# Expert routing by the eight-largest instruction, with fewer rank products and tokens stored in gather order

## The chip, the cores and the metric

The kernel runs on one core of one Trainium2 chip. TensorE multiplies, VectorE and ScalarE (ACT) compute on the fly, GpSimd (POOL) does a few small operations and SyncE (SP) issues nearly all loads. The metric is the device time of one execution in microseconds, the median of three runs.

## The reference

A token block of 256 x 1024 fp32 passes through two layers. The first has a pooling mixer, stick-breaking attention, cross-attention to a memory, gates and a dense feed-forward part. The second has two kinds of attention, gates and a mixture of experts, followed by a last norm. Only the mixture of experts matters here. Each token chooses one of 4 groups, and in that group the two best of 8 experts; its output is the weighted sum of the two.

```python
def hier_moe(h, w_group, b_group, w_expert, b_expert, w1, w3, w2):
    xt = h.reshape(t, d)
    g_logit = (xt @ w_group + b_group).astype(jnp.float32)
    g_prob = jax.nn.softmax(g_logit, axis=-1)
    g_sel = jnp.argmax(g_logit, axis=-1)
    g_w = jnp.take_along_axis(g_prob, g_sel[:, None], axis=1)
    e_logit = (xt @ w_expert + b_expert).astype(jnp.float32).reshape(t, N_GROUPS, EXPERTS_PER_GROUP)
    e_logit = jnp.take_along_axis(e_logit, g_sel[:, None, None], axis=1)[:, 0]
    top_p, top_i = lax.top_k(jax.nn.softmax(e_logit, axis=-1), EXPERT_TOPK)
    gate = g_w * top_p / jnp.sum(top_p, axis=-1, keepdims=True)
    expert = g_sel[:, None] * EXPERTS_PER_GROUP + top_i
    ...
    def expert_block(args):
        xb, e = args
        hid = jax.nn.silu(xb @ w1[e]) * (xb @ w3[e])
        return hid @ w2[e]
    ...
    out = jax.ops.segment_sum(ys[dest] * gate_sorted[:, None], tok_sorted, num_segments=t)
```

There are 32 experts, each with w1 and w3 of 1024 x 512 and w2 of 512 x 1024: three matrices of 2 MB, 192 MB in all.

## The kernel before, in words

Up to about 677 us the kernel works through a list of weight units written by hand (`step_plan`): a unit is loaded by SP, split into a high and a low part, and multiplied in three products (L672 to L674). The mixture of experts follows; all that the change touches lies between these units and the first expert.

Tokens lie on the 128 partitions, in two blocks (`TB`). **Routing.** The "route" steps transpose the last residual times its gain (`n3`, tokens by features) into `n3T`; L853 multiplies it with the 36 routing columns. ACT sums the squares, VectorE adds them up (L1344, L1340), POOL takes the inverse root (L618). VectorE scales the logits (L1686) and then runs one linked chain: each operation waits for the one before it. It finds the best group (helper `first_of`, four operations, which settles ties by the lowest index), hides the other groups' experts, finds the best expert and then the second in the same way, and adds the two masks to `chosen` (L1729), a 0/1 mask of 256 tokens by 32 experts. ACT meanwhile multiplies `n3` by the token's root (L1272, in place) and takes the exponentials of the logits (L1274).

**Ranks.** TensorE, which waits for `chosen` (`route_sel`), counts with five fp32 products how many tokens ahead of each token chose the same expert (`before` is a strict triangle of ones, `ones` a square of ones), and how many tokens each expert has in all (L961 to L965). An fp32 product appears in the trace as two passes, each with a weight load (PEld) and a matmul (PE). VectorE has in the meantime turned the exponentials into gate weights (L1734 to L1743) and then computes `rank` (L1746).

**Experts.** Experts go in quads of four, with 32 slots each. For a quad, VectorE compares ranks with slot numbers into a one-hot matrix (L1768); TensorE gathers the tokens of the quad with 16 fp32 products (L977), whose stationary operand is `n3[:, tb, c:D:KC]`, every eighth feature; ACT and VectorE copy the result to `xg` (L1280, L1778). For each expert TensorE then multiplies with w1 and w3 (L999), transposes (L1004) and multiplies with w2 (L1009); at the quad's end it adds the weighted results into `h` (L1019, L1793). The first quad is written out, the other seven run in a loop. `count_passes` (L1750 to L1753) finds whether an expert has more than 32 tokens and another pass is needed.

**Loads.** SP issues one 2 MB load for each matrix (L560). Experts 0, 1 and 2 are loaded ahead, into places of their own. From expert 3 on, each load waits until the matrix of an earlier expert in the same buffer has been used (`e_w1`, `e_up`, `e_y`), the first of these for expert 0. So the order of work around the change is set by semaphores between five in-order queues, with no planner.

Of the kernel before, what the change touches and what calls it, by code (L numbers as in the profile page):

```python
# [31 lines left out]
P = 128  # L32
# [12 lines left out]
TAKEN = -3e38  # L45
TOPK = T // 4
# [211 lines left out]
def layers_kernel(nc, a, table, windows, out):  # L258
# [32 lines left out]
    gain_rows = [put(f"gain_row{i}", [P, D], F32) for i in range(2)]  # L291
    tab = put("tab", [P, TABLE_W], F32)
# [71 lines left out]
    n3 = nc.alloc_sbuf_tensor_at("n3", [P, TB, D], F32, offset=o_at)  # L364
    n3T = nc.alloc_sbuf_tensor_at("n3T", [P, KC, T], F32, offset=o_at + 8192)
# [16 lines left out]
    masked_e = moe("masked_e", [P, TB, EXPERTS])  # L382
    pick = moe("pick", [P, TB, EXPERTS])
    pick_one = moe("pick_one", [P, TB, EXPERTS])
# [66 lines left out]
    in_route = sem("in_route")  # L451
# [215 lines left out]
    def _(pe):  # L667
# [289 lines left out]
        route_logits(3)  # L957
        pe.wait_ge(route_sel, 1)

        before = const("before")  # L960
# [70 lines left out]
    def _(act):  # L1031
# [270 lines left out]
    def _(dve):  # L1302
# [377 lines left out]
        dve.wait_ge(hg_ready, 4)  # L1680
        dve.wait_ge(sq_ready, 8)
# [11 lines left out]
        def per_token(x, n):  # L1693

            return x.unsqueeze(1).to_broadcast([P, TB, n])

# [3 lines left out]
        def biggest(dst, src, n):  # L1700
            link(v.tensor_reduce(dst, src, AX.X, ALU.max))
# [142 lines left out]
```

## Time and profile before

| | before |
|---|---|
| median of 3 runs | 1166.13 us (1166.05 to 1167.08) |
| the profiled execution | 1163.87 us |
| its span | 1162.0 us |
| mean granted TensorE clock | 0.93 |
| TensorE busy (PE) | 962.2 us, 83% |
| VectorE, ACT, POOL busy | 525.0, 359.8, 46.3 us |
| read from memory | 308.14 MB |

Shares of busy time are means over stages with different limits, so they do not say what bounds the kernel; a matmul's end is modelled. The rows below come from views of the trace of the profiled execution. A row with an idle time in brackets names what ended the wait. A granted clock of 1.00 is 2.4 GHz, 0.50 is 1.2 GHz. The device time is the span and about 2 us around it.

### The profile page before, as it was taken

The page shows a single profiled execution, that of the slowest core. Times are in us where ns is not written, and L with a number is a line of the kernel's source. Part 1 is how long each engine was busy: PE and PEld are TensorE (multiplying, and loading weights), DVE is VectorE, ACT ScalarE, POOL GpSimd, SP SyncE. Part 2 cuts the span into 40 slices and gives each one's busy share as a digit, 9 for nine tenths or more (in the row PEclk, how much of TensorE's full clock was granted, in tenths as well). Part 3 has the DMA queues.
Part 4 walks back from the last instruction along what each step waited for, and adds up shares of the span by engine and source line. Part 5 has one row for each costly group of instructions (what it writes and reads, how often), then busy time and mean ns, then how long its engine had stood idle before and what let it go on. Part 6 is the DMA issues. An engine that isn't in the chain of part 4 may idle for free.

```text
span 1162.0 us, 23578 instructions
## 1 busy us (share of the span) xinstructions
PE 962.2 (83%) x10387; PEld 849.6 (73%) x10387; DVE 525.0 (45%) x859; ACT 359.8 (31%) x541; POOL 46.3 (4%) x43
## 2 busy tenths in 40 slices
PE   5999999889999998999998867767676767676764
PEld 5999999889999987899887866646454545554542
DVE  4546667666565556778875641212020212111112
ACT  4445546453333335343754411010010000001011
POOL 0100001300000000000210200000000000000000
PEclk8999999999999998999999879988898888888887
DMA  9755423736555553455436777999999999999993
GB/s 332 237 170 171 137 73 91 254 130 206 190 180 181 180 182 109 146 156 170 128 128 229 267 301 304 393 420 422 419 422 421 422 422 422 423 423 424 422 421 142
DMA packets 121377, 310.02 MB, mean 267 GB/s; under 512 B 5637, under 2 KB 92361, under 8 KB 113001
## 3 DMA queue, kind: packets, MB, share of 16 engines
q1 hardware_dynamic: 119568, 304.66, 69.9%
q0 software_dynamic: 1008, 4.20, 1.0%
q8 instruction: 43, 0.70, 0.2%
q10 hardware_dynamic: 744, 0.35, 0.1%
q14 instruction: 14, 0.11, 0.0%
HBM read 308.14 MB, written 1.05 MB: 266 GB/s over the span
## 4 chain that ended last, share of the span: by engine, by line
PE 51%; issue 42%; DVE 3%; DMA 2%; ACT 1%; POOL 1%; SPq 0%; ACTq 0%; POOLq 0%; DVEq 0%
PE ps L672 16%; PE ps L674 15%; PE ps L673 15%; DMA arena<-in_w_proj_b 1%; PE ps L927 1%; DVE w_lo L1322 1%; PE ps L838 1%; PE ps L770 0%; PE ps L826 0%; DMA rows<-in_g_mix 0%; PE ps L816 0%; PE ps L805 0%; PE ps L804 0%; DVE h L1412 0%; DVE gates L1488 0%
## 5 line engine op out<-in xcount | busy, mean ns | idle before, releaser
L672 PE MATMUL ps<-x_hi,w_hi 128*128 128x256 f32 x928 | 267.4, 288 | 0.0
L673 PE MATMUL ps<-x_lo,w_hi 128*128 128x256 f32 x928 | 263.4, 284 | 0.0
L674 PE MATMUL ps<-x_hi,w_lo 128*128 128x256 f32 x928 | 263.3, 284 | 0.0
L1322 DVE TENSOR_TENSOR w_lo<-arena,w_hi 128x2048 fp32r<-128x2048 f32 (+3 forms) x83 | 165.5, 1997 | 65.0 <-ACT w_hi L1064 64.3
L999 PE MATMUL ps<-arena,xg 128*32 128x128 f32 x3968 | 137.2, 300 | 62.9 <-DMA arena<-in_w 55.6
L672 PEld LDWEIGHTS ps<-x_hi,w_hi 128*128 128x128 f32 x928 | 178.1, 192 | 5.4 <-issue 4.3
L999 PEld LDWEIGHTS ps<-arena,xg 128*32 128x32 f32 x3968 | 122.8, 121 | 79.7 <-DMA arena<-in_w 66.9
L673 PEld LDWEIGHTS ps<-x_lo,w_hi 128*128 128x128 f32 x928 | 178.1, 192 | 1.6 <-issue 1.0
L674 PEld LDWEIGHTS ps<-x_hi,w_lo 128*128 128x128 f32 x928 | 178.0, 192 | 0.2
L1064 ACT ACTIVATE w_hi<-arena 128x2048 fp32r<-128x2048 f32 (+3 forms) x83 | 138.5, 1671 | 48.9 <-PE ps L674 26.5
L1782 DVE TENSOR_TENSOR hid<-silu_e,ps 128x128 f32<-128x128 f32 x32 | 9.2, 288 | 188.5 <-ACT silu_e L1285 188.5
L1009 PE MATMUL ps<-arena,hid_T 128*32 128x256 f32 x992 | 71.2, 435 | 26.9 <-DMA arena<-in_w 18.8
L672 PE MATMUL ps<-w_hi,x_hi 128*128 128x256 f32 x256 | 76.8, 300 | 11.6 <-DVE w_lo L1322 11.5
L977 PEld LDWEIGHTS ps<-one_hot,n 128*128 128x128 f32 x256 | 61.8, 336 | 25.1 <-DVE one_hot L1768 23.8
L977 PE MATMUL ps<-one_hot,n 128*128 128x128 f32 x256 | 63.3, 424 | 19.2 <-DVE one_hot L1768 19.2
L674 PE MATMUL ps<-w_hi,x_lo 128*128 128x256 f32 x256 | 74.7, 292 | 0.0
L673 PE MATMUL ps<-w_lo,x_hi 128*128 128x256 f32 x256 | 74.7, 292 | 0.0
L1009 PEld LDWEIGHTS ps<-arena,hid_T 128*32 128x32 f32 x992 | 35.6, 123 | 51.9 <-DMA arena<-in_w 23.7
L1787 DVE COPY y_quad<-ps 32x256 f32<-32x256 f32 x64 | 27.2, 425 | 92.9 <-PE ps L1009 91.9
L1332 DVE TENSOR_TENSOR w_lo<-arena,w_hi 128x2048 fp32r<-128x2048 f32 x24 | 55.0, 2293 | 31.2 <-ACT w_hi L1074 31.2
L1285 ACT ACTIVATE silu_e<-ps 128x128 f32<-128x128 f32 x32 | 8.9, 278 | 178.5 <-PE ps L999 178.5
L1288 ACT ACTIVATE y_quad<-ps 32x256 f32<-32x256 f32 x64 | 23.9, 374 | 126.2 <-PE ps L1009 125.4
(274 smaller groups left out, 1330.3 us busy)
## 6 DMA issues: line engine op xcount, KB each, us to landing
arena<-in_w SPq DMA_DIRECT2D x93, 2048.0 KB, 24.0
arena<-in_w_in SPq DMA_DIRECT2D x43, 1024.0 KB, 5.3
arena<-in_w_ffn_in SPq DMA_DIRECT2D x22, 1024.0 KB, 5.1
arena<-in_w_ffn_out SPq DMA_DIRECT2D x11, 1024.0 KB, 4.9
arena<-in_w_out SPq DMA_DIRECT2D x8, 1024.0 KB, 6.1
third_w<-in_w SPq DMA_DIRECT2D x3, 2048.0 KB, 12.6
arena<-in_w_mem_kv SPq DMA_DIRECT2D x2, 1024.0 KB, 5.7
arena<-in_w_pool_o SPq DMA_DIRECT2D x4, 512.0 KB, 3.4
```

The costliest lines, as they stand in the source:

```text
L672: mm(dst, l_hi, r_hi, start=start, stop=False)
L673: mm(dst, l_hi, r_lo, start=False, stop=False)
L674: return mm(dst, l_lo, r_hi, start=False, stop=stop)
L838: mm(o[:, 0:T], v[:, 0, :], r[:, 0:T], start=True, stop=False)
L977: last = mm(ps[:, 2 + c // 4, P * (c % 4):P * (c % 4) + P], n3[:, tb, c:D:KC], one_hot[:, tb, :], start=tb == 0, stop=tb == 1)
L999: last = mm(ps[SLOTS * g:SLOTS * g + SLOTS, 4 + e % 2, P * n:P * n + P], xg[:, c, SLOTS * e:SLOTS * e + SLOTS], places[n][:, c, P * g:P * ...
L1009: last = mm(ps[SLOTS * g:SLOTS * g + SLOTS, 7, 0:UC], hid_T[:, SLOTS * b:SLOTS * b + SLOTS], places[2][:, b, UC * g:UC * g + UC], start=b ...
L1064: fn(w_hi[:, u % 3, 0:n], ring[:, u % 3, 0:n], ACT.Copy).then_inc(hi_ready, 1)
L1288: fn(y_quad[SLOTS * e:SLOTS * e + SLOTS, UC * g:UC * g + UC], ps[SLOTS * g:SLOTS * g + SLOTS, 7, 0:UC], ACT.Copy).then_inc(e_yA, 1)
L1322: v.tensor_tensor(w_lo[:, u % 3, 0:n], ring[:, u % 3, 0:n], w_hi[:, u % 3, 0:n].bitcast(F32), ALU.subtract).then_inc(lo_ready, 1)
L1332: v.tensor_tensor(w_lo[:, s, :], ring[:, s, :], w_hi[:, s, :].bitcast(F32), ALU.subtract)\
L1787: v.tensor_copy(y_quad[SLOTS * e:SLOTS * e + SLOTS, UC * g:UC * g + UC], ps[SLOTS * g:SLOTS * g + SLOTS, 7, 0:UC]).then_inc(e_yD, 1)
```

## The change

- VectorE's chain: the group's mask is turned into 0 or -1e30 and added to the experts' logits. The eight-largest instruction gives each token's best values, the first two are copied into `top2` (padded with -2.5e38), and match-and-replace marks their first places in a copy (`left_e`); a comparison makes `chosen`. The second `first_of` chain is gone. Two memsets for the pads and `slot_no` come ahead of the sum of squares.
- The inputs of the exponential are computed after `chosen`, and the gate weights (`gate_weights`) after the first quad's one-hot.
- TensorE multiplies `ones` by the identity 16 times between the logits and its wait for `chosen`. One rank product covers both token blocks, a second adds the first block's counts to the second's; the two count products come after, in another bank with a semaphore of their own.
- ACT writes the scaled tokens to `n3g`, in the order in which the gather reads its stationary operand. `n3g` lies over columns of the constant table that are no longer needed; `later` changes its place in the table for that. ACT's wait for the transposes (`route_T`) is gone.

```diff
-for _name, _n in (("ident", P), ("later", P), ("before", P), ("rotate", P), ("keep", CAUSAL), ("hide", CAUSAL),
+for _name, _n in (("ident", P), ("before", P), ("later", P), ("rotate", P), ("keep", CAUSAL), ("hide", CAUSAL),
...
+    n3g = nc.alloc_sbuf_tensor_at("n3g", [P, TB, KC, P], F32, offset=tab_at + 4 * TABLE["later"][0])
...
+    masked_e = moe("masked_e", [P, TB, EXPERTS + 6])
+    left_e = moe("left_e", [P, TB, EXPERTS + 6])
+    top2 = moe("top2", [P, TB, 8])
...
         route_logits(3)
+        for _ in range(16):
+            mm(ps[:, 2, 0:P], ones[:, :], ident, start=True, stop=True)
         pe.wait_ge(route_sel, 1)
...
-        mm(ps[:, 1, 0:EXPERTS], before, chosen[:, 0, :], start=True, stop=True)
-        mm(ps[:, 1, EXPERTS:2 * EXPERTS], before, chosen[:, 1, :], start=True, stop=False)
-        mm(ps[:, 1, EXPERTS:2 * EXPERTS], ones[:, :], chosen[:, 0, :], start=False, stop=True)
-        mm(ps[:, 1, 64:64 + EXPERTS], ones[:, :], chosen[:, 0, :], start=True, stop=False)
-        mm(ps[:, 1, 64:64 + EXPERTS], ones[:, :], chosen[:, 1, :], start=False, stop=True).then_inc(rank_done, 1)
+        mm(ps[:, 1, 0:2 * EXPERTS], const("before"), chosen[:, :, :].rearrange("p b e -> p (b e)"), start=True,
+           stop=False)
+        mm(ps[:, 1, EXPERTS:2 * EXPERTS], ones[:, :], chosen[:, 0, :], start=False, stop=True).then_inc(rank_done, 1)
+        mm(ps[:, 5, 0:EXPERTS], ones[:, :], chosen[:, 0, :], start=True, stop=False)
+        mm(ps[:, 5, 0:EXPERTS], ones[:, :], chosen[:, 1, :], start=False, stop=True).then_inc(count_done, 1)
...
-                    last = mm(ps[:, 2 + c // 4, P * (c % 4):P * (c % 4) + P], n3[:, tb, c:D:KC],
+                    last = mm(ps[:, 2 + c // 4, P * (c % 4):P * (c % 4) + P], n3g[:, tb, c, :],
...
         act.wait_ge(root_done, moe_event + 1)
-        act.wait_ge(route_T, 4)
         for tb in range(TB):
-            fn(n3[:, tb, :], n3[:, tb, :], ACT.Copy, scale=stat[:, moe_event, 6 + tb:7 + tb]).then_inc(n3_ready, 1)
+            fn(n3g[:, tb, :, :], n3[:, tb, :].rearrange("t (p c) -> t c p", c=KC), ACT.Copy,
+               scale=stat[:, moe_event, 6 + tb:7 + tb]).then_inc(n3_ready, 1)
...
         dve.wait_ge(hg_ready, 4)
+        v.memset(masked_e[:, :, EXPERTS:], PAD)
+        v.memset(top2[:, :, :], PAD)
+        link(v.tensor_scalar(slot_no[:, :], const("slot"), 1.0, None, ALU.add))
         dve.wait_ge(sq_ready, 8)
...
-        biggest(gmax, lg, GROUPS)
+        link(v.tensor_reduce(gmax, lg, AX.X, ALU.max))
+        tt(pick_g[:, :, :], lg, wide(gmax, GROUPS), ALU.is_equal)
+        tt(pick_g[:, :, :], pick_g[:, :, :], const("revg").unsqueeze(1).to_broadcast([P, TB, GROUPS]), ALU.mult)
+        link(v.tensor_reduce(place, pick_g[:, :, :], AX.X, ALU.max))
+        tt(pick_g[:, :, :], pick_g[:, :, :], wide(place, GROUPS), ALU.is_equal)
+        link(v.tensor_scalar(pick_g[:, :, :], pick_g[:, :, :], 1.0, -NEG, ALU.subtract, ALU.mult))
...
+        tt(real.rearrange("p b (g e) -> p b g e", g=GROUPS), le.rearrange("p b (g e) -> p b g e", g=GROUPS), own,
+           ALU.add)
+        for tb in range(TB):
+            link(v.max(best8[:, tb, :], masked_e[:, tb, 0:EXPERTS]))
+        link(v.tensor_copy(top2[:, :, 0:2], best8[:, :, 0:2]))
+        for tb in range(TB):
+            link(v.match_replace(left_e[:, tb, :], top2[:, tb, :], masked_e[:, tb, :], TAKEN))
+        v.tensor_scalar(chosen[:, :, :], left_e[:, :, 0:EXPERTS], TAKEN / 2 + PAD / 2, None, ALU.is_lt)\
+            .then_inc(route_sel, 1)
+        dve.wait_ge(route_sel, 1)
         tt(exp_in[:, :, 0:GROUPS], lg, wide(gmax, GROUPS), ALU.subtract)
-        first_of(pick_g[:, :, :], lg, gmax, const("revg"), GROUPS, place)
...
-        first_of(chosen[:, :, :], masked_e[:, :, :], best, const("rev"), EXPERTS, place)
...
-        first_of(pick_one[:, :, :], masked_e[:, :, :], second, const("rev"), EXPERTS, place)
-        v.tensor_tensor(chosen[:, :, :], chosen[:, :, :], pick_one[:, :, :], ALU.add).then_inc(route_sel, 1)
-        dve.wait_ge(route_sel, 1)
-        link(v.tensor_scalar(slot_no[:, :], const("slot"), 1.0, None, ALU.add))
...
+        def gate_weights():
...
+            dve.wait_ge(route_exp, 1)
...
         def count_passes():
+            dve.wait_ge(count_done, 1)
...
                 v.tensor_tensor(hot, slots, mine, ALU.is_equal).then_inc(hot_part, 1)
                 dve.wait_ge(hot_part, q * 2 + (tb + 1))
+            if not looped:
+                gate_weights()
```

## Rows read from the trace of the kernel before

**Rows 1.** Page, part 2: the 40 slices of the span, DMA share and rate
```profile
DMA  9755423736555553455436777999999999999993
GB/s 332 237 170 171 137 73 91 254 130 206 190 180 181 180 182 109 146 156 170 128 128 229 267 301 304 393 420 422 419 422 421 422 422 422 423 423 424 422 421 142
```

**Rows 2.** Stretches of the expert stage: us, busy (count) by engine, clock, DMA share, GB/s
```profile
694.00:703.20 9.20, 8.52 (x123) 8.31 (x126) 0.69 (x1) 2.15 (x3) 0.00 (x0) 0.91 0.01 4
749.50:754.00 4.50, 3.31 (x105) 2.79 (x99) 0.58 (x2) 0.28 (x1) 0.00 (x0) 1.00 0.86 277
754.00:1142.50 388.50, 261.89 (x4598) 199.00 (x4587) 64.62 (x162) 32.91 (x93) 0.00 (x0) 0.87 1.01 419
```

**Rows 3.** Waits of the load queue, 676 to 712 us: total, times, longest
```profile
SPq L560 <- PE ps L999: 26.0, 2, 24.6
```

**Rows 4.** Timeline of the routing: start, length, engine, line, form, count, [idle before]
```profile
680.99 0.15 DVE L1344 TENSOR_REDUCE stat<-sq_part 128x2 f32<-128x8 f32 x1
681.13 1.02 PEld L853 LDWEIGHTS ps<-w_route,n3T 128*128 128x128 f32 x8 [1.02 <-DVE n3T L1655]
681.13 1.17 PE L853 MATMUL ps<-w_route,n3T 128*128 128x36 f32 x8 [0.78 <-DVE n3T L1655]
...
681.84 0.70 POOL L618 TENSOR_TENSOR stat<-stat,minus_half 128x2 f32<-128x2 f32 x1 [31.79 <-DVE stat L1340]
682.57 0.55 DVE L1686 SCALAR_TENSOR_TENSOR logits<-ps,stat,b_route 128x36 f32<-128x36 f32 x2 [1.23 <-POOL stat L618]
682.62 2.19 ACT L1272 ACTIVATE n<-n,stat 128x1024 f32<-128x1024 f32 x2 [3.33 <-POOL stat L618]
...
684.83 1.28 ACT L1274 ACT_TABLE_LOAD   x1
...
688.06 0.23 DVE L1729 TENSOR_TENSOR chosen<-chosen,pick_one 128x64 f32<-128x64 f32 x1
...
688.34 0.63 PE L961 MATMUL ps<-chosen,tab 128*128 128x32 f32 x2 [6.04 <-DVE chosen L1729]
688.53 0.16 DVE L1734 TENSOR_REDUCE r_s<-exp_out 128x2 f32<-128x8 f32 x1
...
690.06 0.61 PE L965 MATMUL ps<-chosen,ones 128*128 128x32 f32 x2
...
690.81 0.22 DVE L1746 SCALAR_TENSOR_TENSOR rank<-ps,chosen 128x64 f32<-128x64 f32 x1
691.07 0.62 DVE L1768 TENSOR_TENSOR one_hot<-slot_no,rank 128x128 f32<-128x128 f32 x2
...
691.83 7.88 PE L977 MATMUL ps<-one_hot,n 128*128 128x128 f32 x32 [1.15 <-DVE one_hot L1768]
...
699.75 0.60 ACT L1280 ACTIVATE xg<-ps 128x512 f32<-128x512 f32 x1 [13.37 <-PE ps L977]
```

**Rows 5.** Vector operations by shape: count, busy us, mean ns
```profile
L1673 DVE MAX8 best<-work 128x8 f32<-128x128 f32 x8 | 2.3, 286 | 0.0
L1674 DVE MATCH_REPLACE8 work<-best,work 128x128 f32<-128x128 f32 x8 | 2.2, 276 | 0.0
...
L1552 DVE MEMSET ones<- 128x128 f32 x1 | 0.2, 165 | 0.8 <-PEq L1831 0.8
```

**Rows 6.** Stretches of the routing and of the first gather, columns as in Rows 2
```profile
682.00:688.30 6.30, 0.30 (x2) 0.15 (x1) 4.96 (x24) 3.73 (x4) 0.54 (x1) 0.50 1.00 426
691.80:695.65 3.85, 3.82 (x16) 3.85 (x17) 1.06 (x6) 0.00 (x0) 0.00 (x0) 0.50 0.46 186
695.65:699.70 4.05, 4.05 (x20) 4.04 (x19) 0.00 (x0) 0.00 (x0) 0.00 (x0) 1.00 0.00 0
```

**Rows 7.** Timeline of the second quad, columns as in Rows 4
```profile
739.49 7.91 PE L977 MATMUL ps<-one_hot,n 128*128 128x128 f32 x32 [2.42 <-DVE one_hot L1768]
...
750.53 38.13 SPq L560 DMA_DIRECT2D arena<-in_w  x12
...
789.31 3.67 PE L1019 MATMUL ps<-y_quad,gate_T 128*128 128x512 f32 x8 [1.11 <-DVE y_quad L1787]
```

More of the change, by code:

```diff
@@ L45 @@
 TAKEN = -3e38
+PAD = -2.5e38
 TOPK = T // 4
@@ L1710, in _ @@
-        gmax, place, gsum, best, second, total, share = (r_s[:, i, :] for i in range(7))
-        lg, le = logits[:, :, 0:GROUPS], logits[:, :, GROUPS:36]
-        biggest(gmax, lg, GROUPS)
-        tt(exp_in[:, :, 0:GROUPS], lg, wide(gmax, GROUPS), ALU.subtract)
-        first_of(pick_g[:, :, :], lg, gmax, const("revg"), GROUPS, place)
-        own = pick_g[:, :, :].unsqueeze(3).to_broadcast([P, TB, GROUPS, PER_GROUP])
-        dst, hidden = (t[:, :, :].rearrange("p b (g e) -> p b g e", g=GROUPS) for t in (masked_e, pick))
@@ L1718, in _ @@
-        tt(dst, le.rearrange("p b (g e) -> p b g e", g=GROUPS), own, ALU.mult)
-        link(v.tensor_scalar(hidden, own, 1.0, -NEG, ALU.subtract, ALU.mult))
-        tt(dst, dst, hidden, ALU.add)
-        biggest(best, masked_e[:, :, :], EXPERTS)
-        v.tensor_tensor(exp_in[:, :, GROUPS:36], masked_e[:, :, :], wide(best, EXPERTS), ALU.subtract)\
-            .then_inc(route_in, 1)
-        first_of(chosen[:, :, :], masked_e[:, :, :], best, const("rev"), EXPERTS, place)
-        link(v.scalar_tensor_tensor(masked_e[:, :, :], chosen[:, :, :], 2 * NEG, masked_e[:, :, :], ALU.mult,
-                                    ALU.add))
@@ L1736, in _ @@
-        link(v.tensor_reduce(total, exp_out[:, :, GROUPS:36], AX.X, ALU.add))
-        link(v.reciprocal(total, total))
-        tt(gate_e[:, :, :], exp_out[:, :, GROUPS:36], wide(total, EXPERTS), ALU.mult)
-        tt(gate_e[:, :, :], gate_e[:, :, :], chosen[:, :, :], ALU.mult)
-        link(v.tensor_reduce(share, gate_e[:, :, :], AX.X, ALU.add))
-        link(v.reciprocal(share, share))
-        tt(share, share, gsum, ALU.mult)
-        tt(gate_e[:, :, :], gate_e[:, :, :], wide(share, EXPERTS), ALU.mult)
+        gmax, place, gsum, _, _, total, share = (r_s[:, i, :] for i in range(7))
@@ new lines, in _ @@
+        own = pick_g[:, :, :].unsqueeze(3).to_broadcast([P, TB, GROUPS, PER_GROUP])
+        real = masked_e[:, :, 0:EXPERTS]
+        tt(real.rearrange("p b (g e) -> p b g e", g=GROUPS), le.rearrange("p b (g e) -> p b g e", g=GROUPS), own,
[5 more added lines that the diff above has]
+            link(v.match_replace(left_e[:, tb, :], top2[:, tb, :], masked_e[:, tb, :], TAKEN))
@@ L1747, in _ @@
                                     ALU.mult))
+        def gate_weights():
+            dve.wait_ge(route_exp, 1)
+            link(v.tensor_reduce(gsum, exp_out[:, :, 0:GROUPS], AX.X, ALU.add))
+            link(v.reciprocal(gsum, gsum))
+            link(v.tensor_reduce(total, exp_out[:, :, GROUPS:36], AX.X, ALU.add))
+            link(v.reciprocal(total, total))
+            tt(gate_e[:, :, :], exp_out[:, :, GROUPS:36], wide(total, EXPERTS), ALU.mult)
+            tt(gate_e[:, :, :], gate_e[:, :, :], chosen[:, :, :], ALU.mult)
+            link(v.tensor_reduce(share, gate_e[:, :, :], AX.X, ALU.add))
+            link(v.reciprocal(share, share))
+            tt(share, share, gsum, ALU.mult)
+            tt(gate_e[:, :, :], gate_e[:, :, :], wide(share, EXPERTS), ALU.mult)
         def count_passes():
-            link(v.tensor_reduce(r_s[:, 8, 0:1], ps[:, 1, 64:64 + EXPERTS], AX.X, ALU.max))
+            dve.wait_ge(count_done, 1)
+            link(v.tensor_reduce(r_s[:, 8, 0:1], ps[:, 5, 0:EXPERTS], AX.X, ALU.max))
             link(v.tensor_scalar(exp_in[:, 0, 0:8], const("steps"), r_s[:, 8, 0:1], None, ALU.is_lt))
```

22 lines of the change are left out of this document (4 added, 18 removed).

## The prediction

> **What bounds the kernel now.** I read the 40 slices first, then the waits of the load queue, then the stretches around the one hole they show, and last the timeline of that hole. From slice 27 to slice 39 the memory rate stands near 420 GB/s in nearly every slice [rows 1]: the expert stage lives on its stream of weights. Over its long part, 754.0 to 1142.5 us, the stream moves 419 GB/s at a DMA share of 1.01 while TensorE is busy 262 of 388.5 us [rows 2]. An engine made faster there is worth nothing. What counts is when the stream starts and where it stands still. It stands still once for long: from 694.0 to 703.2 us it moves 4 GB/s [rows 2]. The reason is in the load queue: its longest wait, 24.6 us, is for the up-projection of the first expert (L999) [rows 3]. Experts 0 to 2 were loaded ahead; expert 3 needs the buffers of expert 0, which are free only when routing and first gather are over and expert 0 has run. So every microsecond by which the first gather ends earlier moves the whole stream, as long as the hole is not used up: 9.2 us are there. There is a second, small hole, 749.5 to 754.0 us, at 277 GB/s [rows 2]: the queue waits for the first expert of the second quad, behind that quad's gather [rows 7].
>
> The chain to shorten is therefore [rows 4]: the token statistics (L1344, L618), the vector chain to `chosen` (ready at 688.06 + 0.23 = 688.29), the rank products on TensorE (688.34 to 690.06 + 0.61 = 690.67), rank and one-hot on VectorE (690.81 to 691.69), the gather (from 691.83, 7.88 us), and the copies of its result (from 699.75).
>
> **The change, part by part.** All times are those of the profiled execution: 1163.87 us, of which 1162.0 us are span. The median of the three timed runs is 1166.13, 2.26 us more; I carry the difference over unchanged.
>
> *New work ahead of the statistics.* Two memsets and `slot_no` are now ahead of L1344 on VectorE. L1344 started at 680.99 with nothing between it and the copy before it, so POOL's root and everything behind it move. A memset of 128 columns takes 0.165 us [rows 5]; at most 3 times that, 0.5. They are pure additions, so no gain is possible, and 0 is the other end. I take 0.5: logits start at 683.05 in place of 682.57.
>
> *The vector chain.* Before, from the first logits (682.57) to `chosen` (688.06) lie 23 starts: 0.24 us each [rows 4]. Now two logits are followed by 13 operations: one maximum over groups, four for the group, one turned into a mask, one addition, two eight-largest, one copy, two match-and-replace, one comparison. An eight-largest over 128 columns takes 0.286 and a replace 0.276 [rows 5], over 32 and 38 columns hardly more than the 0.24 of a step; the replace has a separate value load, for which I add 0.1 in all. 14 steps of 0.24, plus 0.23, plus 0.1 make 3.7: `chosen` is ready at 686.75, 1.5 us earlier. At 128-column prices for all four it would be about 0.2 later.
>
> *Sixteen warm-up products on TensorE.* TensorE's queue is in order, so the rank products stand behind them, and the gather behind those. They start when the logit products end, 681.13 + 1.17 = 682.3 [rows 4]. Each is two passes, 32 in all. At 2.4 GHz a pass of this kind takes 0.12 (eight loads in 1.02 us, less the tail of the last) [rows 4]; 128 columns streamed do not take longer (eight products of 512 columns in 3.67 us [rows 7], 0.46 each, a quarter is 0.115). At 1.2 GHz it takes 0.215 (eight passes from 688.34 to 690.06) [rows 4]. So the warm-ups end between 682.3 + 3.8 = 686.1 and 682.3 + 6.9 = 689.2. From 682.0 the granted clock is 0.50, that is 1.2 GHz; TensorE then stood nearly idle, and the clock was full only from 695.65, after 3.85 us of gather [rows 6]. I carry this delay over: 17.7 slow passes until 686.1, the other 14.3 fast in 1.7, end at 687.8. That is after `chosen` (686.75), so about 1.05 us of the vector chain's gain is lost in this queue; a later `chosen` would cost nothing up to there.
>
> *Rank.* Two products (4 passes, 0.5 at 2.4 GHz, 0.86 at 1.2) in place of five before the rank is read: 688.3. The count products come after it; the number of passes is needed only at the end of the first quad. From the last rank product to VectorE's start it took 0.14, from there to the gather 1.02 [rows 4]: the gather starts at 689.45 in place of 691.83, 2.4 us earlier.
>
> *The gather.* Its weights were every eighth element of a token's row; now they are contiguous. Before, 32 passes took 7.88 us, 0.24 each, and the pace did not follow the clock: 3.85 us at 0.50 and 4.05 us at 1.00 hold about the same number of records, 16 and 20, of the latter two already the transposes behind it [rows 6]. So the stride set the pace, not the clock. Contiguous, I take 0.12, in all 3.8 us: 4.1 us gained. Bounds: nothing (another cause of the 0.24), and 4.1.
>
> *Who writes that order.* ACT's two copies (2.19 us, from 682.62) now read with the stride and write in a row. At the old price they end at 685.3, table load at 686.6. The gather asks for them at 689.45. The bound from above is the factor that the stride cost TensorE, 0.24 to 0.12, twice: 4.4 us, end at 687.5. Hidden by 1.9 us. Dropping the wait for the transposes is worth nothing, since the root comes later. The table's columns that are overwritten are no longer read.
>
> The Trainium skill speaks here against the change: "SBUF — State Buffer" (section "Door 1: The DMA port swizzle", its note on cachelines) says that SBUF is read in lines of 16 bytes and that each access to a new line pays, so for fp32 a stride beyond 4 elements costs. The gather's pace agrees with it; that the same penalty meets ACT's copies is not shown by any row of before. If it were twofold, the time would be the same as by the row.
>
> *Moved work.* The exponential is fed two steps after `chosen`, 687.25, and ends near 687.5 behind the table load. The ten gate operations (688.53 to 690.81, 2.3 us [rows 4]) now come behind the one-hot, from 689.3; with the two gated one-hots and the four of the pass count VectorE is free at about 693.0, and the gather ends at 689.45 + 3.8 = 693.25. Covered, but only by 0.25 us: if the gather is faster than I think, its result waits here. No DMA issue is moved and none is passed by another.
>
> *Sum.* 2.4 + 4.1 = 6.5 us, less than the 9.2 us of the hole, so it passes in full to the stream. Second quad: the small hole costs (419 - 277) x 4.5 / 419 = 1.5 us of stream [rows 2]. The second gather (7.91 us [rows 7]) gets 1.0 us shorter if all passes are slow, 4.1 if all are fast, 2.4 with the clock's delay of 3.85 us: 1.5 of it closes the hole. In the other six quads the stream covers it. Together 8.0 us: 1155.9 in a profiled execution, **1158.1** against the median.
>
> The clock alone moves this. With the warm-ups ending at 686.1, `chosen` governs, and the gather starts at about 688.5: 0.95 more. With an end at 689.2 it starts at about 690.85: 1.4 less. Its own range is thus 1157.0 to 1159.7. The Trainium skill, "TensorE: Matmul & The Clock Gate", Part 1, holds that the number of slow products after a start differs between runs of one kernel; one profiled execution can't show that.
>
> **The rivals.**
> *The clock stays at 1.2 GHz.* Warm-ups to 689.2, ranks in 0.86, gather from 691.2 and in 6.9 us: ends at 698.1 in place of 699.71, 1.6 gained, and 1.0 in the second quad. Time: 1163.5. For it: after the five rank products the clock was still at 0.50. Against it: a solid stretch brought it back, after 3.85 us [rows 6].
> *The new order does not quicken the gather.* The 0.24 would then be a matter of the product itself. 2.4 are gained: 1163.7. Against it: the 0.12 of the other products on the same data width.
> *The stream gives it back.* If later stretches are limited by something other than the bytes, the earlier start ends in a longer wait: 1166.1, no change. Against it: 419 GB/s over 388 us.
> *Slower: ACT's strided copies.* The mechanism is their reading; the place is TensorE's wait for both ahead of the first gather. From 689.45 on they delay the gather one for one. The whole 8.0 us are lost when they end at 697.5, 14.4 us after their start at 683.1, 7.2 us for one copy in place of 1.1; at 8.6 us for one it is 1169.0. For it: no row shows ACT reading such a stride. Against it: the same stride cost TensorE a factor of two.
>
> **How the numbers follow.** Forecast 0.70; slow clock 0.11; gather not quicker 0.09; given back 0.06; slower 0.04. From all of this I can tell only what exceeds 0.2%, 2.3 us. The forecast is faster; of the two rivals at 2.6 and 2.4 us of gain about two thirds, 0.14, would be told as faster; the rest and the third are the same. So faster 0.84, same 0.12, slower 0.04. The range reaches from the forecast's fast end, with half a microsecond for the tail behind the last load, to the slow clock: 1156.4 to 1163.5.
>
> **What would show it.** The chain right: gather start near 689.5 and passes near 0.12 at full clock; the hole of 9.2 us shrunk to about 2.7; no stretch near 277 GB/s in the second quad; the same 419 GB/s after it. Wrong: warm-ups that end after 689 at clock 0.50; passes still at 0.24; ACT's copies over 3 us each; VectorE still in the gate weights when the gather ends; a hole that opens at a later quad.

## The result and the profile after

The changed kernel takes 1158.28 us in the median of five runs (1152.85 to 1159.67), the kernel before 1166.13 (1165.64 to 1167.08): a ratio of 0.9929 with an interval of 0.9905 to 0.9954. The forecast was 1158.1. The runs of the changed kernel lie 6.8 us apart, those of before 1.4 (in the later comparisons, of 16 or 17 runs, 4.4 to 6.8), and the profiled execution is the changed kernel's lowest, 1152.85 us with a span of 1151.0. The trace therefore shows more gain than the median, and the difference has to be explained too.

Page after, part 2, answering to [rows 1]. The dip before the plateau is nearly gone; the plateau is the same.

```profile
DMA  9754423746555553545444889999999999999993
GB/s 334 226 184 142 152 67 109 229 137 209 183 182 182 184 186 113 160 142 167 147 145 154 288 327 367 419 419 422 422 421 421 422 421 422 423 423 423 421 423 152
```

Stretches after, answering to [rows 2, 6]: start:end, length, busy (count) of PE, PEld, DVE, ACT, POOL, granted clock, DMA share, GB/s.

```profile
681.50:684.70 3.20, 3.20 (x16) 3.20 (x16) 1.87 (x10) 2.12 (x2) 0.70 (x1) 0.50 0.99 425
684.90:692.40 7.50, 6.89 (x63) 6.80 (x61) 5.24 (x28) 3.48 (x3) 0.00 (x0) 1.00 0.98 409
693.20:696.20 3.00, 2.88 (x107) 2.91 (x111) 0.02 (x1) 1.41 (x2) 0.00 (x0) 1.00 0.10 36
705.20:736.00 30.80, 23.35 (x453) 17.72 (x457) 8.17 (x20) 3.66 (x10) 0.00 (x0) 1.00 1.01 421
736.00:743.00 7.00, 5.81 (x173) 4.91 (x168) 1.42 (x4) 1.03 (x3) 0.00 (x0) 1.00 1.01 408
743.00:1131.50 388.50, 250.50 (x4517) 180.96 (x4506) 63.14 (x158) 32.08 (x91) 0.00 (x0) 0.86 1.01 420
```

The hole of 9.2 us at 4 GB/s is now one of 3.0 us at 36. The second hole, 277 GB/s before, is gone (408). The stream behind it is the same, 420 against 419. The load queue's longest wait fell accordingly, from 24.6 us [rows 3] to this one (total, times, longest):

```profile
SPq L564 <- PE ps L1004: 28.3, 4, 17.6
```

Timeline of the routing after, answering to [rows 4]: start, length, engine, line, form, count, [idle before].

```profile
680.92 0.16 DVE L1349 TENSOR_REDUCE stat<-sq_part 128x2 f32<-128x8 f32 x1
...
682.03 5.16 PE L963 MATMUL ps<-tab,ones 128*128 128x128 f32 x32
682.52 0.55 DVE L1694 SCALAR_TENSOR_TENSOR logits<-ps,stat,b_route 128x36 f32<-128x36 f32 x2 [1.23 <-POOL stat L622]
682.58 4.26 ACT L1276 ACTIVATE n3g<-n,stat 128x1024 f32<-128x1024 f32 x2 [3.60 <-POOL stat L622]
...
684.56 0.42 DVE L1718 MAX8 best<-masked_e 128x8 f32<-128x32 f32 x2
...
685.81 0.20 DVE L1722 TENSOR_SCALAR chosen<-left_e 128x64 f32<-128x64 f32 x1
...
687.02 0.33 PE L966 MATMUL ps<-chosen,tab 128*128 128x64 f32 x2
...
687.59 0.22 DVE L1730 SCALAR_TENSOR_TENSOR rank<-ps,chosen 128x64 f32<-128x64 f32 x1 [1.12 <-PE ps L968]
...
688.61 3.81 PE L982 MATMUL ps<-one_hot,n3g 128*128 128x128 f32 x32 [0.61 <-DVE one_hot L1767]
...
691.88 0.15 DVE L1752 CAST passes_i<-r_s 128x1 int32<-128x1 f32 x1
...
692.46 0.60 ACT L1285 ACTIVATE xg<-ps 128x512 f32<-128x512 f32 x1 [4.04 <-PE ps L982]
692.53 0.69 DVE L1779 COPY xg<-ps 128x512 f32<-128x512 f32 x1 [0.49 <-PE ps L982]
...
695.33 2.07 SPq L564 DMA_DIRECT2D arena<-in_w  x2
```

The last line is the first load of expert 3, at 695.33. VectorE was done with the gate weights 0.49 us before the gather ended.

**A clock that two executions share.** The work up to the loads of expert 2 (`third_w`, issued by SP) is the same in both kernels, yet it ends at 673.98 to 678.99 us in the 14 profiles of this case. I therefore count from that issue, t0: 676.72 before, 676.42 after. The table gives, in us after t0, when each event starts (the end of the span in the last column); "last w2 product" is the last group of products with a w2 matrix.

| kernel | gather starts | its copies | w1 of expert 3 | last w2 product | end |
|---|---|---|---|---|---|
| before | 15.11 | 23.03 | 25.90 | 465.80 | 485.28 |
| before, again | 15.11 | 23.03 | 25.90 | 465.75 | 485.15 |
| changed | 12.19 | 16.04 | 18.91 | 456.60 | 474.58 |
| changed, again | 12.20 | 16.05 | 18.91 | 456.65 | 474.71 |
| changed, third | 12.19 | 16.04 | 18.90 | 460.55 | 478.56 |

Within a kernel the routing and the gather come at the same time to 0.01 us; between the kernels they differ by 7.0 us. What follows varies more.

### The profile page after: what moved, and what is told of

Same layout as the page of the kernel before. It is cut to its first block, busy times and chain, and to the rows that moved or that the text cites. A ratio compares the mean times of both kernels' runs of the same rounds, so it can differ in the third digit from the quotient of the medians.

```text
span 1151.0 us, 23634 instructions
## 1 busy us (share of the span) xinstructions
PE 948.4 (82%) x10417; PEld 829.9 (72%) x10417; DVE 522.5 (45%) x856; ACT 361.5 (31%) x541; POOL 46.3 (4%) x43
## 4 chain that ended last, share of the span: by engine, by line
PE 52%; issue 41%; DVE 3%; ACT 1%; DMA 1%; POOL 1%; ACTq 0%; POOLq 0%; DVEq 0%; SPq 0%
PE ps L676 16%; PE ps L677 15%; PE ps L678 15%; PE ps L931 1%; DMA arena<-in_w_proj_b 1%; DVE w_lo L1327 1%; PE ps L842 1%; PE ps L830 0%; PE ps L774 0%; DMA rows<-in_g_mix 0%; PE ps L820 0%; PE ps L809 0%; PE ps L808 0%; DVE h L1417 0%; DVE gates L1493 0%
## 5 line engine op out<-in xcount | busy, mean ns | idle before, releaser
L1004 PE MATMUL ps<-arena,xg 128*32 128x128 f32 x3968 | 141.4, 306 | 66.2 <-DMA arena<-in_w 60.2
L1004 PEld LDWEIGHTS ps<-arena,xg 128*32 128x32 f32 x3968 | 125.4, 124 | 86.6 <-DMA arena<-in_w 75.2
L1014 PE MATMUL ps<-arena,hid_T 128*32 128x256 f32 x992 | 76.3, 457 | 35.4 <-DMA arena<-in_w 29.6
L676 PEld LDWEIGHTS ps<-w_hi,x_hi 128*128 128x128 f32 x256 | 52.0, 203 | 14.6 <-DVE w_lo L1327 12.2
L1079 ACT ACTIVATE w_hi<-arena 128x2048 fp32r<-128x2048 f32 x24 | 45.8, 1910 | 49.9 <-PE ps L678 49.9
```

The lines of the kernel that those rows point to most:

```text
L676: mm(dst, l_hi, r_hi, start=start, stop=False)
L1004: last = mm(ps[SLOTS * g:SLOTS * g + SLOTS, 4 + e % 2, P * n:P * n + P], xg[:, c, SLOTS * e:SLOTS * e + SLOTS], places[n][:, c, P * g:P * ...
L1014: last = mm(ps[SLOTS * g:SLOTS * g + SLOTS, 7, 0:UC], hid_T[:, SLOTS * b:SLOTS * b + SLOTS], places[2][:, b, UC * g:UC * g + UC], start=b ...
L1079: fn(w_hi[:, s, :], ring[:, s, :], ACT.Copy).then_inc(hi_ready, 1)
```

## The experiments

Each kernel below is the changed one with one edit, or the one before with one part of the change. Kernels that were timed together share one set of runs of the kernel before. Its median is 1164.19 for the changed kernel again, the order undone, the first version without warm-ups and the order alone; 1164.41 for the delay, the first early version and the repetitions of the changed kernel and of the one without warm-ups; 1164.49 for the other four.

### The changed kernel again

No edit.

> The changed kernel once more, for a second profile and five more times. Its first profile has a span of 1151.0 us, while the other four runs have spans of 1155.6 to 1157.9. If the stream theory holds in the ordinary run too, the first gather ends near 692.4 and the hole of the load stream is near 3 us in this profile also; a longer span must then show a second place where the stream stands still or TensorE waits (candidate: waits marked 'issue' in the first quad, of which before had 2.8 us and the first profile of after 0.6 us). Rival: the spread comes from the clock, and the warm-ups end later, near 689. Median 1157 to 1159.

Measured: median 1155.51 of 6 (1151.07 to 1158.47), ratio 0.992 (0.9899 to 0.9941). The gain is 8.7 us here, 7.85 in the first comparison; the chain comes at the same times after t0. The spread of some 7 us is there again.

### The gather's order undone

```diff
-                    last = mm(ps[:, 2 + c // 4, ...], n3g[:, tb, c, :],
+                    last = mm(ps[:, 2 + c // 4, ...], n3[:, tb, c:D:KC],
...
+        act.wait_ge(route_T, 4)
...
-            fn(n3g[:, tb, :, :], n3[:, tb, :].rearrange("t (p c) -> t c p", c=KC), ACT.Copy,
...
+            fn(n3[:, tb, :], n3[:, tb, :], ACT.Copy, ...
```

> The changed kernel with the tokens left in n3 and gathered with the stride again; all else as changed. Stream theory: the first gather takes 7.9 us in place of 3.8, the whole stream is 4.1 us later, the second quad's hole reopens (about 1.5 us): near 1163.9, that is 5.6 above the changed kernel. Rival (the earlier routing carries the gain, the gather is hidden by the stream): within 1.5 us of the changed kernel.

Measured: median 1161.01 of 12 (1155.36 to 1163.3), ratio 0.9963 (0.9948 to 0.9978). Timeline of this kernel, then its stretch of the gather:

```profile
682.73 2.19 ACT L1277 ACTIVATE n<-n,stat 128x1024 f32<-128x1024 f32 x2 [3.58 <-POOL stat L622]
...
688.78 7.86 PE L982 MATMUL ps<-one_hot,n 128*128 128x128 f32 x32 [0.61 <-DVE one_hot L1767]
```

```profile
688.80:696.60 7.80, 7.80 (x34) 7.80 (x34) 2.93 (x16) 0.00 (x0) 0.00 (x0) 1.00 0.61 246
...
738.00:750.00 12.00, 10.05 (x217) 8.92 (x220) 2.08 (x5) 1.89 (x5) 0.00 (x0) 1.00 1.01 418
```

At full clock throughout the strided gather takes 7.86 us, as before with half of it at 0.50. So the stride sets its pace, not the clock. Against the changed kernel's first profile the order is worth 4.05 us at the gather's end (20.09 against 16.04 after t0), at expert 3's load (22.96 against 18.91), at the last product (460.65 against 456.60) and 4.1 at the end. I had added the second hole to the order's account; in this kernel that hole is closed as well (418 GB/s), with the strided gather. So the order isn't what closes it. The faster routing need not be either: TensorE has none of the idle stretches in the first quad that the kernel before has there (1.29 and 1.54 us, below). The medians lie 5.5 us apart, and the intervals of the two ratios don't meet (0.9948 and more here, 0.9941 and less there).

### The warm-ups left out, twice

```diff
-        for _ in range(16):
-            mm(ps[:, 2, 0:P], ones[:, :], ident, start=True, stop=True)
```

> The changed kernel without the 16 warm-up products. The rank products then start when chosen is ready (686.05) at 1.2 GHz, 4 passes in 0.86, and the gather at about 688.1, half a us earlier than with warm-ups, but slow until the clock returns 3.85 us later: 17.7 passes at 0.215 and 14.3 at 0.12, end near 693.6 against 692.4. Clock theory: 1.2 us slower than the changed kernel, near 1159.5. Rival (the warm-ups are only a delay in TensorE's queue): 0.5 us faster. Second rival (the clock stays low through the first expert too): 4 us slower or more.

> One more look at the kernel without the 16 warm-ups. Its first profile had the third experts' loads at 674.0, the first load of expert 3 20.1 later (18.9 with warm-ups) and the end 478.6 later (474.7 with them), with waits marked 'issue' of 1.21, 0.42 and 0.16 in the first quad and a stretch at 1.2 GHz there. If the warm-ups are worth 4 us in the stage, this profile again has 478 to 479 from these loads to the end. Rival (the 4 us were a chance of the clock): 475 to 476.

Stretches of the first profile without warm-ups (its first gather, then two places in the first quad), then the first gather of its repetition:

```profile
685.70:689.30 3.60, 3.56 (x17) 3.59 (x18) 2.91 (x15) 0.17 (x1) 0.00 (x0) 0.53 1.00 408
689.30:691.20 1.90, 1.90 (x19) 1.83 (x17) 0.16 (x2) 0.01 (x1) 0.00 (x0) 1.00 0.77 313
706.00:709.50 3.50, 3.50 (x49) 2.47 (x45) 0.51 (x2) 0.52 (x2) 0.00 (x0) 0.52 1.01 413
711.00:714.00 3.00, 2.00 (x68) 1.47 (x56) 0.20 (x1) 0.28 (x1) 0.00 (x0) 1.00 0.81 198
```

```profile
689.40:693.20 3.80, 3.80 (x18) 3.80 (x19) 3.07 (x16) 0.11 (x1) 0.00 (x0) 0.51 0.99 399
693.20:695.00 1.80, 1.80 (x18) 1.77 (x17) 0.00 (x0) 0.00 (x0) 0.00 (x0) 1.00 0.74 303
```

The ranks come 1 us earlier (9.65 after t0, not 10.60), the gather's first 17 passes are slow, and it takes 5.41 and 5.61 us; its copies start 1.2 and 1.4 us later than with warm-ups. So much was expected. Behind it, t0 to end is 478.6 in both profiles, 4.0 more than in two of the changed kernel's three profiles and the same as in its third. Of the 4.0, 2.3 and 2.4 are there when the last w2 product starts (458.94 and 459.04); the rest is that product itself, which takes 3.55 and 3.45 us and not 1.93. The share ahead of that product is more than the gather's 1.2 and 1.4: in the first quad the clock is at 0.52 for 3.5 us, and behind it the stream falls to 198 GB/s for 3 us. The median is 1154.8 (1153.41 to 1160.35, ratio 0.9929, 0.9907 to 0.995), 0.7 *under* that of the changed kernel in the same comparison; the single run of the repetition was 1157.96. The warm-ups gain 1.2 to 1.4 us at the gather; that the time gains by it isn't shown.

The Trainium skill ("TensorE: Matmul & The Clock Gate", Part 1) has the number of slow products after a start vary from run to run. Here it varies too, by little: in the two profiles without warm-ups the clock was back 3.4 and 3.8 us after the gather's start, and the gathers took 5.41 and 5.61 us.

### The order alone in the kernel before

```diff
...
+    n3g = nc.alloc_sbuf_tensor_at("n3g", [P, TB, KC, P], F32, offset=tab_at + 4 * TABLE["later"][0])
...
-                    last = mm(ps[:, 2 + c // 4, ...], n3[:, tb, c:D:KC],
+                    last = mm(ps[:, 2 + c // 4, ...], n3g[:, tb, c, :],
...
-            fn(n3[:, tb, :], n3[:, tb, :], ACT.Copy, ...
+            fn(n3g[:, tb, :, :], n3[:, tb, :].rearrange("t (p c) -> t c p", c=KC), ACT.Copy, ...
```

> The kernel before with only the new order of the tokens (ACT writes n3g, the gather reads it), routing as before. Stream theory: the gather starts at 691.8 at 1.2 GHz and takes about 5.5 us in place of 7.9, 2.4 earlier, and 1.5 in the second quad: near 1162.2, 3.9 under the kernel before. Rival (the order is worth its full 4.1 plus 1.5 without the warm-ups): near 1160.5. Rival (no effect without the earlier routing): 1166. ACT's copies take about 2.1 us each and are over at 686.9, hidden.

Measured: median 1159.25 of 6 (1158.41 to 1162.02), ratio 0.9953 (0.9939 to 0.9968); in the profile the last w2 product and the end come 3.4 us earlier after t0. Timeline, then the gather's stretches:

```profile
684.19 4.16 ACT L1274 ACTIVATE n3g<-n,stat 128x1024 f32<-128x1024 f32 x2 [3.34 <-POOL stat L620]
...
693.40 5.66 PE L979 MATMUL ps<-one_hot,n3g 128*128 128x128 f32 x32 [1.16 <-DVE one_hot L1771]
```

```profile
693.40:697.00 3.60, 3.60 (x17) 3.60 (x18) 1.03 (x6) 0.00 (x0) 0.00 (x0) 0.50 0.48 196
697.30:699.10 1.80, 1.80 (x18) 1.75 (x16) 0.00 (x0) 0.00 (x0) 0.00 (x0) 1.00 0.00 0
```

A contiguous pass takes 0.21 us at 0.50 (3.60 / 17) and half of that at 1.00. The order alone thus cuts the gather by 2.2 us (7.88 to 5.66) and starts expert 3's load 2.2 earlier. The other 1.85 of its 4.05 need the clock, which came up only during this gather.

### A delay put in: 48 warm-ups

```diff
-        for _ in range(16):
+        for _ in range(48):
```

> The changed kernel with 48 warm-up products in place of 16: a pure delay of the rank products by 64 passes at 2.4 GHz, 0.12 each, 7.7 us. It measures what a delay of the first gather is worth at the end. Stream theory: first use of expert 3's load, last landing and end each move by about 7.7 us against the changed kernel (from the issue of the third experts' loads: 18.9 to 26.6, 456.6 to 464.3): median 7 to 8 above the changed kernel, as slow as the kernel before. Rival (the stream gives it back): under 2 us above the changed kernel.

Timeline, then the hole:

```profile
684.64 12.26 PE L963 MATMUL ps<-tab,ones 128*128 128x128 f32 x96
...
698.33 3.81 PE L982 MATMUL ps<-one_hot,n3g 128*128 128x128 f32 x32 [0.61 <-DVE one_hot L1767]
```

```profile
697.50:705.30 7.80, 6.51 (x120) 6.22 (x123) 4.38 (x20) 2.15 (x3) 0.00 (x0) 1.00 0.01 2
```

The 64 added passes delay the gather by 7.15 us (19.34 against 12.19 after t0), 0.112 each, less than the 0.12 I had taken. Expert 3's load comes 7.1 later, the last product 7.2, the end 7.2; the median is 1161.75 of 12 (1157.76 to 1166.37), 6.2 over the changed kernel's 1155.51 (in the same comparison it ran once, 1155.52). The stream passes a delay through the hole one for one. "The stream gives it back" falls as a rule of this kernel.

### Expert 3's first matrix loaded early, twice

w1 of expert 3 gets a place of its own, where the tokens and their transposes lay, and no longer waits for expert 0. Expert 4's loads, which the loop holds back until expert 2 has used its matrices, wait only for expert 1, whose buffers they take. Expert 5's are written out too, with the wait that they had (expert 3).

```diff
+    fourth = nc.alloc_sbuf_tensor_at("fourth_w1", [P, 2, UNIT], F32, offset=o_at)
...
+    fourth_w1 = fourth[:, :, :].rearrange("p s (c n) -> p (s c) n", c=KC // 2)
...
-        for which in range(3):
-            sp.wait_ge((e_w1, e_up, e_y)[which], 1)
-            expert_load(3, odd_w, which, landed_w[1][which])
+        sp.wait_ge(logit_done, 1)
+        sp.wait_ge(n3_ready, 2)
+        expert_load(3, [fourth_w1], 0, landed_w[1][0])
+        for which in range(1, 3):
+            sp.wait_ge((e_up, e_y)[which - 1], 1)
+            expert_load(3, odd_w, which, landed_w[1][which])
+        for e, used in ((4, 2), (5, 4)):
+            for which in range(3):
+                sp.wait_ge((e_w1, e_up, e_y)[which], used)
+                expert_load(e, (even_w, odd_w)[e % 2], which, landed_w[e % 2][which])
...
-        stream(0, 2)
+        stream(0, 3)
...
-                    places = (odd_w, even_w, third_w, odd_w)[e]
+                    places = (odd_w, even_w, third_w, [fourth_w1, odd_w[1], odd_w[2]])[e]
```

> The changed kernel, with w1 of expert 3 loaded into the space of n3 and n3T as soon as ACT has copied the tokens and the logits are done, and with expert 4's loads waiting for expert 1 (whose buffers they use) and no longer for expert 2. In the changed kernel the stream stands still for 3.0 us before the first expert's buffers are free (693.2 to 696.2, 36 GB/s). Stream theory: the 5 us load fills this, the last landing is 3 us earlier (from the issue of the third experts' loads: 456.6 to 453.6 or a little less), median near 3 us under the changed kernel. Rival (TensorE's own time in the first two quads is by now as long as the stream's): under 1 us gained.

> The version with w1 of expert 3 loaded early, three more rounds and a second profile, beside the two kernels above on the same chip. Last landing 453.3 after the third experts' loads within 0.5, whatever waits TensorE has in the first quad; median 1152 to 1154, 3 us under the changed kernel and 11 to 12 under the kernel before.

Timeline of the load queue in the first of the two, then the stretch that was the hole:

```profile
678.03 1.28 SPq L566 DMA_DIRECT2D third_w<-in_w  x3
688.57 0.33 SPq L566 DMA_DIRECT2D fourth_w<-in_w  x1
```

```profile
693.30:696.30 3.00, 2.32 (x61) 2.11 (x63) 1.00 (x3) 2.15 (x3) 0.00 (x0) 1.00 1.07 437
```

Of the two parts of the edit only the second was also timed alone (below). The load goes out at 10.5 us after t0, when ACT has read the tokens, and where the hole was the stream moves 437 GB/s; a dip of 2 us at 254 GB/s is left where the next load starts (699 to 701 us). The last product comes 3.3 and 2.9 us earlier than in the changed kernel, as much as the hole was long. Medians 1152.5 of 6 (1147.96 to 1155.16, ratio 0.9894, 0.9871 to 0.9918) and 1152.42 of 4 (1149.94 to 1155.21, ratio 0.9902, 0.9879 to 0.9925): 12 us under before and 3 under the changed kernel, whose interval overlaps these. These are the lowest medians found.

### The spread: the changed kernel and the kernel before, profiled again

No edit in either, one run each (1155.52 and 1165.54). The question was whether the spread comes only from the code ahead of t0.

> One more look at the changed kernel, for the spread of its runs. Two profiles of it have the third experts' loads at 676.4 and then 474.6 and 474.7 us to the end. If the spread comes from the stages ahead of the change, this profile's span differs by what the issue of these loads differs, and the time from there to the end stays at 474.6 within 0.5. Rival (it comes from the expert stage, by the clock at the tail or waits in the first quad): the issue is at 676.4 again and the rest differs by up to 4.

> The kernel before, one more look. Its first profile has two waits of TensorE marked 'issue' in the first quad, 1.29 and 1.54 us, and 36.1 us from the first load of expert 3 to the second quad's one-hot, where the cleanest run of the others (old order, no such wait) has 32.7. If these waits are a lottery of each execution, this profile has another set of them, and the time from the third experts' loads to the end is 485.3 shifted by about what that stretch differs. Rival (they are fixed by the code): the same two waits within 0.3 us, and 485.3 within 0.5. Routing and gather as before in both (15.1 and 23.0 after those loads, the gather's end up to 1.5 off by the clock).

The changed kernel's third profile has t0 1.3 us *earlier* than the first, but a span 2.7 longer. Its stretches, then two rows of TensorE's timeline, where "issue" is idle time for which the profile shows no releaser:

```profile
701.70:703.60 1.90, 0.00 (x0) 0.00 (x0) 0.00 (x0) 0.00 (x0) 0.00 (x0) 1.00 0.98 414
704.10:710.60 6.50, 5.33 (x67) 3.19 (x63) 0.58 (x2) 0.28 (x1) 0.00 (x0) 0.50 0.96 397
711.30:714.20 2.90, 2.22 (x84) 1.95 (x77) 0.64 (x2) 0.54 (x2) 0.00 (x0) 1.00 0.03 13
```

```profile
703.69 2.18 PE L1004 MATMUL ps<-arena,xg 128*32 128x128 f32 x39 [2.04 <-issue]
...
713.23 2.17 PE L1004 MATMUL ps<-third_w,xg 128*32 128x128 f32 x72 [0.68 <-issue]
```

Every engine stood idle for 1.9 us while loads ran at 414 GB/s. Then the clock was at 0.50 for 6.5 us, experts 1 and 2 were late, and with them the loads of expert 4, which wait for expert 2: a new hole of 2.9 us at 13 GB/s. The last product comes 3.95 us later than in the first profile. So the spread doesn't lie ahead of t0 alone; here 4 of the 7 us were given back behind the first hole.

For the kernel before I had expected waits that differ from one profile to the next. They hardly do. TensorE's issue rows of the first profile, then of the second:

```profile
712.32 0.49 PE L999 MATMUL ps<-arena,xg 128*32 128x128 f32 x9 [1.29 <-issue]
720.17 1.50 PE L999 MATMUL ps<-third_w,xg 128*32 128x128 f32 x42 [1.54 <-issue]
```

```profile
714.35 0.49 PE L999 MATMUL ps<-arena,xg 128*32 128x128 f32 x9 [1.48 <-issue]
722.20 1.50 PE L999 MATMUL ps<-third_w,xg 128*32 128x128 f32 x42 [1.53 <-issue]
```

Same places, nearly the same lengths, and t0 to end 485.28 and 485.15, though t0 itself lies 1.8 us apart (676.72 and 678.55). As far as two profiles go, the kernel before varies ahead of t0 alone.

### Only expert 4's wait relaxed

```diff
+        for e, used in ((4, 2), (5, 4)):
+            for which in range(3):
+                sp.wait_ge((e_w1, e_up, e_y)[which], used)
+                expert_load(e, (even_w, odd_w)[e % 2], which, landed_w[e % 2][which])
-        stream(0, 2)
+        stream(0, 3)
```

> The changed kernel with only the wait of expert 4's loads relaxed (expert 1 in place of expert 2). In one of three profiles of the changed kernel TensorE stood still for 2.0 us in the first quad, ran at 1.2 GHz after it, and the stream stood still a second time for 4 us (711 to 715), since expert 4's loads waited for expert 2. If that second hole is what the slow runs of the changed kernel pay, its median here falls by 1 to 2 us against the changed kernel (near 1154) and the slowest runs go; a clean run is as before, 474.6 from the third experts' loads to the end. Rival (the second hole comes from elsewhere): no difference from the changed kernel, 1155.5, and the profile shows a hole between 710 and 716 whenever it shows such a wait.

TensorE's two longest issue rows, then the stretch that holds them:

```profile
706.71 1.30 PE L1008 MATMUL ps<-arena,xg 128*32 128x128 f32 x39 [1.32 <-issue]
716.05 2.17 PE L1008 MATMUL ps<-third_w,xg 128*32 128x128 f32 x72 [3.07 <-issue]
```

```profile
704.00:720.00 16.00, 9.23 (x259) 7.40 (x253) 2.01 (x6) 1.30 (x4) 0.00 (x0) 1.00 1.01 420
```

Waits of 1.32 and 3.07 us, the second longer than any above, and yet 420 GB/s and a last product at 456.70: with the looser rule, they cost the stream nothing in this profile. The clock stayed at 1.00 here, so the case with a slow clock was not met. In time no gain shows: 1155.92 of 11 (1150.94 to 1162.47), ratio 0.993 (0.991 to 0.995), where I had expected a lower median and no run as slow as 1162.47. So that the changed kernel's slower runs come from expert 4's wait isn't shown.

### The early version without warm-ups

The edit of the early version and that of the left-out warm-ups together.

> The version with w1 of expert 3 loaded early, without the 16 warm-ups. The gather ends 1.2 us later than with them (20.1 to 20.3 in place of 18.9 to the first free buffer), but the stream has a load of 5 us to move in that time, against a hole of 3.0 + 1.2: hidden, median 1152.5 within 1. Rival (the warm-ups also keep TensorE's clock up in the first quad): 2 us or more slower than with them.

Measured: median 1155.85 of 6 (1155.11 to 1158.0), ratio 0.9932 (0.9917 to 0.9948), 3.4 over the early version of the same comparison, with intervals that overlap a little. TensorE's longest issue row, then stretches:

```profile
708.35 0.42 PE L1011 MATMUL ps<-arena,xg 128*32 128x128 f32 x7 [2.02 <-issue]
```

```profile
710.30:713.30 3.00, 3.00 (x32) 1.77 (x36) 0.00 (x0) 0.00 (x0) 0.00 (x0) 0.50 1.07 446
741.00:745.00 4.00, 3.19 (x108) 2.73 (x97) 0.35 (x2) 0.28 (x1) 0.00 (x0) 1.00 0.68 194
```

I had taken a gather that is 1.2 us later for hidden behind the early load. In this profile the time is not kept: the first quad ends later, after a wait and a stretch at 0.50, and the stream opens a hole of 4 us at 194 GB/s behind the second quad's gather, which starts from copies 3 us later than in the early version (61.79 against 58.07 and 58.61 after t0). The gather accounts for 1.5 of these 3 us; how much of the rest is due to the missing warm-ups one profile can't tell. All three profiles without warm-ups have such a wait with a slow stretch behind it; of the seven with 16 warm-ups only one has, the changed kernel's third. That speaks for the rival of the expectation, without showing how.

## Why the prediction was right

It was right in the sum and in the main mechanism: a chain that ends earlier moves the stream, as far as the hole goes. The shares were less right, and the reason for the 1.5 us at the second quad was not the one that I gave.

- **Head.** 0.5 us for the memsets and `slot_no`; it was a quarter. L1349 starts 4.50 us after t0, L1344 4.27 [rows 4], and the logits come at 6.10 instead of 5.85.
- **Vector chain.** 3.7 us from the logits to `chosen`; 682.52 to 686.01 is 3.5. Both eight-largest take 0.42 together; at 32 columns they cost no more than a step.
- **Warm-ups, the term that was mis-sized.** I let the clock come back 3.85 us after they start. They started at 682.03, and the clock was at 0.50 until about 684.8, 2.8 us: some 13 slow passes (2.8 / 0.215) rather than 17.7. The range that I gave for the clock alone was also added up wrongly: 0.95 less and 1.4 more than 1158.1 make 1157.2 to 1159.5, not 1157.0 to 1159.7. The rank product ran from 687.02, 10.60 us after t0; by my sum it would have been 687.8, 11.08. This 0.48 is nearly all of the 0.54 by which the gather starts earlier after t0 than predicted (12.19, not 12.73). The queue was still the later of the two, as predicted: `chosen` was ready at 686.01.
- **Gather.** 3.8 us predicted, 3.81 measured; the stride was the reason (the experiment with the order undone). Its copies start 7.0 us earlier after t0; my sum was 6.5, and the difference is that half a microsecond of the clock.
- **ACT's copies.** They took 4.26 us for both, 2.19 before [rows 4]: a factor of 1.95, just under the bound of two. The note on cachelines that the prediction weighed against the change ("SBUF — State Buffer" in the Trainium skill, section "Door 1: The DMA port swizzle") agrees with ACT's time too. ACT's copies end at 686.84 and the gather starts at 688.61; the slower rival falls. They are also why the early load can't go out before 10.5 us after t0.
- **Cover of the gate weights.** VectorE waited 0.49 us for the gather; I had 0.25.
- **Through the hole.** 7.0 at the copies, 7.0 at expert 3's load. The hole left is 3.0 us; I said 2.7.
- **Second quad.** I took 1.5 us for the 277 GB/s stretch. The last product comes 9.2 us earlier, 2.2 more than the 7.0. Of these, the closed hole is 1.3: its 1.5 less (420 - 408) x 7 / 420 = 0.2 for what the same place still loses. The other 0.9 I had missed: the first quad before, with its two issue waits, moved 387 GB/s over 11.8 us, (420 - 387) x 11.8 / 420 = 0.9, and now that quad runs at 421. My reason for the 1.5 us, a second gather that is shorter by 2.4, isn't needed. It did get shorter, by 4.1 us (7.91 to 3.84), but with the gather's order undone the last product also comes 2.2 us more ahead than the first gather's copies do (5.15 against 2.94). What that kernel and the changed one have in common is a first quad with at most 0.6 us of issue waits in their first profiles, where before has 2.8. That these waits are the cause fits but was not isolated, so here the sum was right by luck. The row of before:

```profile
712.20:724.00 11.80, 7.81 (x187) 6.00 (x190) 2.01 (x6) 1.30 (x4) 0.00 (x0) 1.00 0.97 387
```

- **Tail.** Another 1.5 us of the profiled difference lies outside the prediction: the last w2 product, 32 passes, took 3.43 us before and 1.93 after. The second profile of before and the other two of the changed kernel repeat this (3.32; 1.93 and 1.93), but within the early version it falls either way (3.64 and 1.93). Whether the change brings it isn't shown.

So the profiled gain from t0 is 7.0 + 2.2 + 1.5 = 10.7 us, 485.28 less 474.58. In the third profile it is 6.7, because 4 are given back in the first quad. The medians, 7.85 and 8.7 us of gain, lie between. The forecast of 8.0 met the middle of at least two outcomes, neither of which it had described, and that it came so close is luck. That the stream gives it back was a rival at 0.06, with "419 GB/s over 388 us" against it; the rate did hold, but from 743 us on, and the loss was in the 20 us before.

**Left open.** What the issue waits are. The instruction queue (q8 of the page) moved 0.02 MB shortly before nearly every one, as at 701.0 in the changed kernel's third profile, where the wait begins at 701.65; but it did so without a wait behind it as well (at 700.0, 705.8 and 712.0 in its first). No experiment separated that from the rest. Whether the warm-ups are worth their 16 products in the changed kernel isn't settled either: its medians with and without agree, and only in the early version did leaving them out cost 3.4 us, with intervals that overlap. The faster vector chain and the fewer rank products were not timed apart either; the kernel with the gather's order undone shows what both are worth together with the warm-ups, 2.9 us at the gather.

## What to carry to other kernels

When a stream of loads bounds a stage, look for where it stands still, follow what the load queue waits for, and shorten that chain: it pays one for one until the hole is used up, as the put-in delay showed from the other side. A stationary operand read with a stride can cost a factor of two (7.86 us against 3.81 here) that the full clock doesn't give back; if another engine copies that operand anyway and has slack, let it write the order that is read. And look behind the hole: a wait rule that is uniform for the sake of a loop (expert 4 waiting for expert 2) can pass a small stall on to the stream, as one profile here shows, though relaxing it alone gained nothing that could be measured; and a load that needs only free space need not wait for the chain at all.

## What the runs showed of the hardware that was not expected

- TensorE stands idle for 0.15 to 3.1 us in the first quad with no releaser in the profile, in 12 of the 14 profiles. In the kernel before, these waits are the same in two profiles (1.29 and 1.54, 1.48 and 1.53); in the changed one they differ (0.58; 1.13; 2.04 and 0.68). In six profiles (the third of the changed kernel, both without warm-ups, the early version without them, the order alone, the 48 warm-ups) a wait of 1.1 to 2.0 us is followed by a stretch at clock 0.50; in the one with the longest waits, 1.32 and 3.07, in both of the kernel before and in the changed kernel's second (1.13) none is.
- A pass of 128 columns with strided weights takes 0.24 us at either clock; with contiguous ones 0.21 at 0.50 and 0.112 at 1.00 (the 64 added passes). With strided weights the slow clock cost nothing.
- The clock came back 2.7 to 2.8 us after the warm-ups' start, and 3.4 to 4.1 after that of a gather that started cold (six profiles); the warm-ups came straight behind eight passes for the logits.
- Work that no edit touches ended 5 us apart over 14 profiles. Differences of spans below that say nothing until they are counted from a common event.
